# A decoder-layer kernel on one core: q and k transposed one k-step later, directly ahead of the value products

## The reference

```python
h = rms_norm(x) * (1 + scale) + shift            # shift, scale, gate from silu(c) @ w_ada
q, k, v, gate_a, u, gate_b = split(h @ w_in)      # 8 query heads, 2 key/value heads of 64
q, k = rope(rms_norm(q)), rope(rms_norm(k))
y_a = sliding_window_attention(q, k, v, sinks) * silu(gate_a)   # blocks of 128 queries
y_b = conformer_conv(u) * silu(gate_b)            # GLU, 31-tap causal conv, layer norm, swish
out = x + gate * (concat(y_a, y_b) @ w_out)
```

## Time and profile before

| | us |
|---|---|
| median of 3 runs | 500.44 |
| lowest and highest of them | 499.86, 501.35 |
| the profiled execution's own time | 500.72 |
| its span (first to last instruction) | 499.0 |
| PE busy | 427.4 (86%) |
| PE weight loads busy | 330.5 (66%) |
| DVE busy | 340.5 (68%) |
| ACT busy | 203.4 (41%) |
| POOL busy | 130.8 (26%) |

### The profile page before, as it was taken

The page is one execution under the profiler, slowest core; times in us unless marked ns, Lnnn a source line. Parts: engine busy times, 40 slices in busy tenths (PEclk is TensorE's granted clock), DMA queues, the critical chain, the costliest instruction groups (busy, mean ns, idle before and its releaser), DMA issues.

```text
span 499.0 us, 5645 instructions
## 1 busy us (share of the span) xinstructions
PE 427.4 (86%) x2025; PEld 330.5 (66%) x2025; DVE 340.5 (68%) x558; ACT 203.4 (41%) x442; POOL 130.8 (26%) x137
## 2 busy tenths in 40 slices
PE   0368989999999889999799978973597998999996
PEld 0257776887888777777567745751274776888885
DVE  0689777399997588888856893899642599522222
ACT  5234538221510277677839754230044378210000
POOL 1442020001512233434224187420010173410000
PEclk9999899999999999999979989987598999999999
DMA  7999727204940000040035598452007005991111
GB/s 243 290 271 324 230 74 224 83 0 96 233 67 7 0 12 8 1 133 1 3 83 96 99 143 129 42 128 40 1 29 139 2 0 184 260 249 45 42 43 63
DMA packets 62279, 51.38 MB, mean 103 GB/s; under 512 B 19161, under 2 KB 57101, under 8 KB 62252
## 3 DMA queue, kind: packets, MB, share of 16 engines
q1 hardware_dynamic: 46348, 41.59, 28.0%
q0 software_dynamic: 15904, 9.44, 14.4%
HBM read 46.82 MB, written 4.19 MB: 102 GB/s over the span
## 4 chain that ended last, share of the span: by engine, by line
PE 54%; DVE 29%; issue 6%; ACT 4%; SPq 2%; DMA 2%; POOL 2%; DVEq 0%; ACTq 0%
PE pm L558 6%; PE pm L560 5%; PE pm L559 5%; PE pm L742 4%; DVE cacc L1250 3%; PE pm L744 3%; PE pm L743 3%; PE pm L825 3%; PE pm L824 3%; PE ps L677 3%; PE pm L826 3%; DVE z L1257 2%; PE tr L824 2%; PE tr L825 2%; PE tr L826 2%
## 5 line engine op out<-in xcount | busy, mean ns | idle before, releaser
L558 PE MATMUL pm<-h,wts 128*128 128x512 f32 x224 | 94.1, 420 | 11.7 <-DVE gb L1383 4.0
L560 PE MATMUL pm<-h,wts 128*128 128x512 f32 x224 | 90.3, 403 | 0.0
L559 PE MATMUL pm<-h,wts 128*128 128x512 f32 x224 | 90.0, 402 | 0.0
L558 PEld LDWEIGHTS pm<-h,wts 128*128 128x128 f32 x224 | 43.6, 195 | 28.8 <-issue 10.4
L432 POOL DMA_DIRECT2D wts<-in_w_in x22 | 28.7, 1909 | 86.6 <-ACT wts L884 86.6
L560 PEld LDWEIGHTS pm<-h,wts 128*128 128x128 f32 x224 | 43.6, 195 | 9.7
L559 PEld LDWEIGHTS pm<-h,wts 128*128 128x128 f32 x224 | 43.8, 196 | 9.2 <-issue 0.7
L742 PE MATMUL pm<-wts,h 128*128 128x256 f32 (+1 forms) x128 | 46.0, 359 | 3.6 <-DVE rot L1339 3.4
L882 ACT ACTIVATE wts<-raw 128x1024 fp32r<-128x1024 f32 x30 | 31.2, 1051 | 42.7 <-PE pm L560 14.9
L744 PE MATMUL pm<-wts,h 128*128 128x256 f32 (+1 forms) x128 | 43.1, 337 | 0.0
L743 PE MATMUL pm<-wts,h 128*128 128x256 f32 (+1 forms) x128 | 43.0, 336 | 0.0
(11 more groups left out here) (198 smaller groups left out, 907.9 us busy)
## 6 DMA issues: line engine op xcount, KB each, us to landing
raw<-in_w_in SPq DMA_DIRECT2D x18, 512.0 KB, 6.2
slab<-in_w_ada SPq DMA_DIRECT2D x16, 512.0 KB, 7.4
xs<-in_x SPq DMA_DIRECT2D x8, 512.0 KB, 6.2
raw<-in_w_ada SPq DMA_DIRECT2D x8, 512.0 KB, 4.4
xr<-in_x SPq DMA_DIRECT2D x8, 512.0 KB, 4.3
out<-xr SPq DMA_DIRECT2D x16, 256.0 KB, 2.0
wts<-in_w_in POOLq DMA_DIRECT2D x6, 512.0 KB, 7.6
raw<-in_w_in SPq DMA_DIRECT2D x16, 128.0 KB, 3.7
```

The source lines that it names most:

```text
L558: pe.matmul(out, hi_w, hi_x, start=first, stop=False)
L559: pe.matmul(out, lo_w, hi_x, start=False, stop=False)
L560: return pe.matmul(out, hi_w, lo_x, start=False, stop=last)
```

## The change

`transpose_qk(new)` moves from s = 5 to s = 6, and stands ahead of `times_v(old)` there. The order on PE in rounds 4 to 9 was transposes, k-step 5, value products, k-step 6, k-step 7, scores; it becomes k-step 5, transposes, value products, k-step 6, k-step 7, scores. In rounds 2 and 3, which have no value products, it was transposes, k-steps 5, 6, 7, scores and becomes k-step 5, transposes, k-steps 6, 7, scores. Rounds 10 and 11 have no transposes of q and k. No instruction is added or removed, and no wait is changed.

```diff
             def attention_step(n, s):
                 new, old = n - 2, n - 4
-                if 0 <= old < NT:
-                    if s == 0:
-                        transpose_p(old)
-                    if s == 6:
-                        times_v(old)
+                if 0 <= old < NT and s == 0:
+                    transpose_p(old)
+                if 0 <= new < NT and s == 6:
+                    transpose_qk(new)
+                if 0 <= old < NT and s == 6:
+                    times_v(old)
                 if 0 <= new < NT:
-                    if s == 5:
-                        transpose_qk(new)
                     if s == 8:
                         scores(new, 0)
                     if s == 12:
```

## The result

The changed kernel takes 502.02 us, median of 20 runs (499.75 to 505.21), against 499.85 for the kernel before, also 20 runs, taken beside it (498.11 to 501.35). The ratio is 1.0049, 95% interval 1.0031 to 1.0068: slower by 2.4 us, between 1.5 and 3.4. Forecast were 2.5 us above before. The runs of the changed kernel scatter more widely than those of before, 5.5 us from lowest to highest against 3.2; the experiments show a part of the reason.

What follows compares the result with a forecast made beforehand. The prediction took a circle of PE's transposes, DVE's rotary work and PE's bank wait to bound rounds where DVE is late. 1.36 + 0.41 + 0.64 + 0.08 = 2.49 us gave 502.9 us, range 500.9 to 504.2.

Steps and rivals of the forecast that it cites:

- PE and DVE in a circle: Transposes, DVE's rotary work, PE's bank wait, k-steps bind rounds 2 and 3; each loses 0.68 us, 1.36 together.
- Round 4: PE reaches the k/v tile without idle; slack 0.27 us against DVE 0.68 later, so 0.41 us lost.
- DVE's later queue: Rounds 4 to 8: DVE gets its lateness back in waits for ACT's copy of the scores; one is 1.31 us.
- Rounds 5 to 8: Bank-wait slack of 0.86 us covers the 0.68; PE's own order costs 0.16 a round, 0.64 us in all.
- the direct step: Last transpose straight into value products, rounds 5 to 8: 0.38 us taken, 0.11 the other bound; +0.16 a round.
- DVE's lateness costs nothing: Rounds 5 to 8: the slack of 0.86 us covers DVE being 0.68 later, leaving only PE's own order.
- the 0.08 for round 9: No rotary work follows; value products start at 273.18 instead of 273.10, +0.08 us, bounds 0 and +0.08.
- It reaches the end: The loss before round 10 passes through the convolution to the layer norm, which comes 2.49 us later.
- absorbed: Rival: later slack of DVE or ACT eats the longer circle, convolution ends as before; about 500.6 us, chance 0.14.
- Short step: Rival: transposes run into value products in 0.11 us, rounds 5 to 8 gain 0.44; 501.8 us, chance 0.22.
- Clock lost: Rival: round 2's idle, grown to 2.24 us, makes the clock fall, 2.8 us more; 505.7 us, chance 0.08.
- Clock kept: Rival: the clock falls behind the 3.13 and 3.00 us waits are spared; 498.7 us, chance 0.05.

Runs made afterwards that it cites:

- key copy first: Changed kernel with DVE's first key copy ahead of one convolution tap: 503.63 us, ratio 1.0078 against the kernel before.
- the early transposes: Kernel before with the transposes at s = 2 in round 2 and s = 3 in round 3: 498.40 us, ratio 0.9965.
- the early kernels: Kernel before with transposes at s = 2 and 3 in rounds 2 and 3, without or with round 1's two taps behind the rotary work: ratios 0.9965 and 0.9913.
- rounds 5 to 9 only: Kernel before with the transposes moved to s = 6 in rounds 5 to 9 alone: 500.24 us, ratio 1.0001.
- changed, again: The changed kernel run once more without an edit: 504.31 us, ratio 1.0081 against the kernel before.
- rounds 2 to 4: Kernel before with the transposes moved to s = 6 in rounds 2 to 4 alone: 503.24 us, ratio 1.0065.
- one-round runs: Kernel before with the transposes at s = 6 in round 2 alone, or round 3 alone: 501.43 and 500.23 us, ratios 1.0042 and 1.0029.
- taps behind: Changed kernel with the two convolution taps moved from between DVE's rotary instructions to behind them: 501.73 us, ratio 1.0031 against the kernel before.
- round 3 only: Kernel before with the transposes moved to s = 6 in round 3 alone: 500.23 us, ratio 1.0029.
- double dose: Kernel before with the transposes at s = 7 in rounds 2 and 3, s = 5 elsewhere: 504.23 us, ratio 1.0083.

## Why the prediction was right, point by point

**PE and DVE in a circle.** Right. Moving one k-step ahead of the transposes in round 2 or in round 3 costs 0.66 and 0.67 us each; 1.36 were forecast for both together, 1.33 came.

**Round 4.** 0.41 us were forecast from a slack of 0.27. The bank wait of 0.35 is that part: to the tile the round lost 4.72 + 0.68 - 4.99 = 0.41. But the scores at s = 12 wait 0.21 more for DVE's key copy. Measured from transposes to transposes the round takes 14.20 us instead of 13.53: 0.67. The step that failed is the one that said DVE's later queue gets its lateness back in waits for ACT's copy of the scores. DVE does get it back later in the round; but its first key copy is already late, and PE waits for that in the same round. With the key copy first the round takes 13.94, the 0.41 of the forecast.

**Rounds 5 to 8.** The slack of 0.86 us on the bank wait held: no bank wait in these rounds. The sum had 0.16 us a round for the direct step. That term was mis-sized: the value products start 194.72 - 194.52 = 0.20 behind the last transpose in round 4, and 0.20 or 0.21 in rounds 5 to 8, between the bounds 0.11 and 0.38, and nearer to the one I had not taken. By 0.90 - 0.20 = 0.70 it pays the k-step of 0.68 in full, so PE's order costs nothing. What does cost 0.10 us a round in rounds 5 and 6 is the key copy again: 208.29 to 222.77 and to 237.26 from transposes to transposes, 14.48 and 14.49 where it was 14.39 and 14.38. The run with the key first shows that it was this and not the step. So the prediction's sentence that DVE's lateness costs nothing in these rounds failed too.

**The number, in part by luck.** The errors nearly cancelled: 1.36 + 0.41 + 3 x 0.16 = 2.25 us to round 8 were forecast, and 2.17 came, which is 0.66, 0.66 and 0.67 in rounds 2, 3 and 4 and 0.2 in rounds 5 and 6, within rounding. Of the 0.16 for round 8 and the 0.08 for round 9 nothing is seen: from the transposes of round 8 to those of round 9 it takes 17.02 us against 17.00, and the value products of round 9 start 0.71 behind the first transpose instead of 1.41, so they pay for the k-step. And the second set of runs of the same kernel had a median of 504.31 us, above the range.

**It reaches the end.** Right, as far as the traces tell. Eight of the profiles show one fall of about the same length in round 8 (a granted clock of 0.66 to 0.70 over the 5 us from its start). There the stretch from round 8 to the layer norm's first product took about the same time, 105.27 to 105.59 us, though they had taken between 94.63 and 103.41 to get there. The changed kernel's is 105.59, the one with the early transposes 105.27. The ratios of the early kernels show it in time too. What was won or lost before round 8 isn't taken up, so *absorbed* falls.

**Short step.** It is neither this rival nor the forecast. The rival was nearer in the step itself (0.11 and 0.38, measured 0.20). In what rounds 5 to 7 cost to round 8 the forecast was nearer: it had +0.48, the rival -0.33, and the run with rounds 5 to 9 only measured +0.16, which is about the wait for the key copy. The Trainium skill, page "TensorE: Matmul & The Clock Gate", section "Part 2: What happens when you issue a matmul", says that PE can pull a weight load ahead of matmuls still in flight. In the changed kernel's trace the load of the value products does not go ahead; it starts with the product:

```profile
194.72 0.20 PEld L699 LDWEIGHTS pv<-pcur,v 128*64 128x64 f32 x4 [0.17 <-issue]
```

**Clock lost.** I had put this at 0.08 and said that it decides between an idle of 2.24 and one of 2.43 us. It doesn't decide by one idle: with idles of 2.24 and 1.82 us the clock fell twice in two profiles (changed, again; rounds 2 to 4) and not at all in the first one of the changed kernel. Neither the kernel before nor those with only one of the two idles lengthened showed it. The one-round runs have one profile each, so they don't exclude it. Nor are idles of that length needed: the changed kernel with the taps behind had one fall in round 3, behind idles of 0.63 us ahead of the tile and 1.62 ahead of the scores. What exactly makes the clock fall stays open. It fits that three of the changed kernel's 20 runs lie 2.7 us and more above its median and that its two medians differ by 2 us. That each of those long runs had such falls was not seen, since only one execution of each experiment is profiled, and falls in rounds 2 to 4 are not the only source of scatter: the profiled execution of round 3 only took 502.95 us, 2.7 above its own median, without such a fall; its clock was down for longer in round 8, and the stretch from there took 106.80 us.

**Clock kept.** The waits of 3.13 and 3.00 us are there as before, 3.11 and 3.01. The fall in round 8 was spared in two profiles (changed, again; rounds 2 to 4), and these are the two with falls in rounds 2 and 3 behind idles of 2.24 and 1.82 us; with the double dose, whose clock fell in rounds 2 and 3 as well, it was not spared. So this rival's mechanism occurs, but in some executions only.

**Why single spans mislead.** The clock also falls in round 8, behind the 3.1 us wait for the weights, in most profiles, but for different lengths. The same stretch in the kernel before, in the changed kernel and in the changed kernel again:

```profile
245.00:262.00 17.00, 13.87 (x53) 9.36 (x52) 11.09 (x21) 8.61 (x29) 6.58 (x6) 0.80 0.25 63
```

```profile
245.00:262.00 17.00, 13.89 (x68) 9.87 (x67) 11.75 (x22) 9.88 (x32) 6.58 (x6) 0.90 0.25 63
```

```profile
245.00:262.00 17.00, 13.87 (x84) 10.17 (x83) 13.32 (x24) 11.87 (x35) 6.58 (x6) 1.00 0.25 63
```

From round 8 to the layer norm they took 106.78, 105.59 and 103.89 us. So 1.2 us of the 2.17 lost before round 8 came back by the clock in the one execution that was profiled, and another 1.8 behind the layer norm's first product (granted clock 1.00 behind 400 us, where before had 0.98), while the part ahead of the first mark took 0.3 longer. That makes the span 0.5 us shorter than before. Twenty runs average over this, but the two sets of the same kernel still differ by 2 us.

## What to carry to other kernels

Where two engines wait for each other once a round, moving work from behind the hand-over to ahead of it lengthens every round in which the other engine ends last, by the whole of what was moved, however much idle the first engine has elsewhere. Work out for every wait in the round, not only for the first, how far behind the hand-over it is released: a branch that has no idle today, because another wait covers it, takes over as soon as that one moves. And hand over early where the other engine is late; here the early transposes won 2.8 us to round 8, where the late ones lost 2.2.

## What the runs showed of the hardware that I had not expected

A moderate idle can make the granted clock fall in some executions of the same kernel and not in others: with idles of 2.24 and 1.82 us it stayed at 1.00 in one profile and fell twice in another, which cost 2.7 us up to round 8, of which 1.7 came back because the fall in round 8 did not come. The float32 value products started 0.20 us behind the last of five transposes in rounds 4 to 8 and 0.28 in round 9, where the float32 products of the kernel's first stage started 0.38 behind theirs in five of six places. A change of 0.68 us in a wait thus moved the time through its own length and, in some of the profiled executions, through the clock as well.
